# Copying the scan's output gates out of PSUM before their sigmoid and product

## The chip, the cores and the metric

The kernel runs on one core of a Trainium2 chip. Time is what one execution takes on the device, in microseconds (us). The engines are TensorE (PE, its weight loads PEld), VectorE (DVE), ScalarE (ACT), GpSimd (POOL), and SyncE (SP), which here issues transfers.

## The reference

Two blocks of two layers each work on 512 tokens of width 1024 (and 256 context tokens). What the change touches is the gated linear attention of the second block. Cut to that:

```python
def gla_scan(q, k, v, g, s0):              # once forwards, once backwards
    def step(s, inp):                      # chunks of 128 tokens
        qc, kc, vc, gc = inp
        b = jnp.cumsum(gc, axis=2)
        inter = einsum('bhtd,bhde->bhte', qc * exp(b), s)
        att = einsum('bhtd,bhsd,bhtsd->bhts', qc, kc, exp(rel))
        o = inter + einsum('bhts,bhse->bhte', att, vc)
        ...
y_gla = gla_finish(ol_f + flip(ol_b), o_norm) * jax.nn.silu(g_g)     # g_g = h @ w_in[..., 2336:2848]
m = (jax.nn.sigmoid(ga) * (ya @ w_br_attn)
     + jax.nn.sigmoid(gg) * (yg @ w_br_gla)
     + jax.nn.sigmoid(gs) * (ys @ w_br_sgu))
```

The output gate is silu(g_g) = g_g * sigmoid(g_g), with g_g of 512 features, which are four tiles of 128 features in each layer. The merge gates ga, gg and gs are of 1024 features each.

## The kernel before, in words

Activations lie with features on partitions and tokens in columns: 768 columns in the first of the second block's layers (called layer 0, `L = 0`), 512 in the second (`L = 1`). A projection tile is 128 output features. Its weights arrive by a transfer into one of three `stage` buffers, ACT rounds them to a high half (`whi`, `Weights.hi`, L198), and DVE takes the rest as a low half (`wlo`, `Weights.lo`, L212). PE then runs three products of 8 matmuls for each stretch of columns (high by U high, high by U low, low by U high; L388). The rounding runs four tiles ahead, so the rounding that belongs to a step waits (`w_used`) until PE is through with this step's own tile.

`Banks` gives out PSUM by the program's order. A claim makes PE wait until the event named by the claimant before has happened in the same banks. During the scan, banks 0 to 5 go to the scan's own products (two groups of three banks, `trio`), and every projection tile gets the one slot that is left, banks 6 and 7. So a projection tile can start only when the tile before it has been read out.

The scan of each layer (`pe_gla`, `act_gla`, `dve_gla`, `pool_gla`) works for `f` = 0, 1 (a pair of heads each) through seven levels `lv`. For a level, DVE and POOL take differences (L1884, L1965), ACT takes their exponentials (L1780), DVE and POOL multiply with q and k (L1890, L1972), PE multiplies the two (the `g0t,g0ts` matmuls, with g1 in layer 1), and DVE places the result under a mask (L1900). Between the levels' matmuls on PE lies a *step*, a projection tile that has nothing to do with the scan and fills PE's time. `scan_steps` lays down which tile stands at which place. There are 24 steps in a layer:

- 20 *fill steps* (merge gates). ACT rounds the weight tile ahead, copies the result from PSUM to the one buffer `FS` (L1717, event `fill`) and sends it to DRAM (`GS`, event `spill`). The next projection waits for `fill`.
- 4 *gate steps*, at levels 2 and 4 of each `f`, with the output gates. ACT rounds the weight tile ahead, then applies the sigmoid from PSUM (L1713, event `g_sig`), and DVE multiplies it with the same PSUM tile (L1728, event `g_gate`). The next projection waits for `g_gate`.

PE's order is level, step, level, step. Behind the matmuls of a step stand the matmuls of the next level in other banks, and only then the next step's. The product `g0g` / `g1g` is read only when `f` is finished (L1914).

Of the kernel before, what the change touches and what calls it, by code (L numbers as in the profile page):

```python
# [11 lines left out]
ALU = mybir.AluOpType  # L12
ACT = mybir.ActivationFunctionType
# [14 lines left out]
def _layout():  # L28
# [19 lines left out]
SHARED = {event: kind for kind, events in {  # L48
    "u_hi": ("n_hi", "m_uhi", "e_hi"), "u_lo": ("n_lo", "m_ulo", "e_lo"),
    "y_hi": ("f_hi", "s_yhi", "g_yhi", "q_yhi", "v_yhi"), "y_lo": ("f_lo", "s_ylo", "g_ylo", "q_ylo", "v_y"),  # L50
    "h_new": ("res", "b_add", "e_r", "h_final"), "evicted": ("m_qk", "s_qk", "q_z", "fill", "g_qk", "g_af", "v_x"),
    "modulated": ("n_mul", "u_mod"), "gain": ("n_gain", "u_gain"), "rows_act": ("m_va", "g_va"),
    "rows_dve": ("m_vd", "g_vd", "s_v", "q_v"), "v_norm": ("v_blo", "v_st", "v_ag", "v_rr", "v_n", "v_n1", "v_n2"),
    "qk_norm": ("q_rr", "q_nz"), "sigmoid": ("cb_sig", "cb_moved", "b_sig", "q_gs", "v_sig", "g_sig", "m_o"),
# [12 lines left out]
class Signals:  # L67
# [13 lines left out]
    def up(self, name, *key, by=1):  # L81
        kind = SHARED.get(name, name)
        self.count[kind] = self.count.get(kind, 0) + by
        if self.built:
            assert self.value[(name,) + key] == self.count[kind], (name, key)
        else:
            assert (name,) + key not in self.value, (name, key)
            self.value[(name,) + key] = self.count[kind]
        return self.handle(name), by

    def dma(self, name, *key):
        return self.up(name, *key, by=16)

    def at(self, name, *key):
        return self.handle(name), self.value[(name,) + key] if self.built else 1
# [127 lines left out]
def scan_steps():  # L223


    places = [("kd", m) for m in range(4)]
    for f in range(2):
        places += [("lv", f, lv) for lv in range(7)] + [("end", f, i) for i in range(3)]
    early = [(tag, j) for tag in "gas" for j in range(8)]
    tiles, gates = {}, {}  # L230
    for place in places:
        if place[0] == "lv" and place[2] in (2, 4):
            tiles[place] = ("p_gg", 2 * place[1] + place[2] // 4, None)
        else:
            n = len(gates)
            tag, j = early[n]
            gates[(tag, j)] = n
            tiles[place] = ("p_m" + tag, j, n)
    return tiles, gates


STEPS, EARLY = scan_steps()


def weight_plan():
# [62 lines left out]
def trunk_kernel(nc, A, out, stop=None):  # L308
    ctx = ExitStack()
    with ctx:  # L310
# [9 lines left out]
        def wide(name, offset, n=TOK):  # L320
            return place(name, [128, n], F32, offset)[:, :]
# [32 lines left out]
        def T(name, i):  # L354
            return number[(name, i)]

        S = Signals(lambda name: ctx.enter_context(nc.semaphore("s_" + name)))
        up, dma, at = S.up, S.dma, S.at
        B = Banks(S, PS)
        W = Weights(S, [A[name][i, :, :] for name, i in plan], plan, stage, parts)  # L360
# [41 lines left out]
        def pe_tile(pe, i, s, x, nk, full, sub=0, width=128, xt=None):  # L402
            wh, wl = W.views(i, nk)
            if sub == 0:
                pe.wait_ge(*at("w_lo", i))
            last = None
            if xt:
                for k in range(nk):
                    pe.wait_ge(*at(*xt[k]))
                    for a, b in cols(full):  # L410
                        for q, (xr, wv) in enumerate(((0, wh), (1, wh), (0, wl))):
                            last = mm(pe, s[:, a:b], wv[:, k, sub:sub + 128], x(xr, k, a, b), k + q == 0,
                                      k == nk - 1 and q == 2)
                return last
            for a, b in cols(full):
                n = 0
                for xr, wv in ((0, wh), (1, wh), (0, wl)):
                    for k in range(nk):
                        last = mm(pe, s[:, a:b], wv[:, k, sub:sub + 128], x(xr, k, a, b), n == 0, n == 3 * nk - 1)
                        n += 1  # L420
            return last

        def pe_proj(pe, i, x, full, *until, xt=None):
            s = B.take(pe, i, *until)
            pe_tile(pe, i, s, x, 8, full, xt=xt).then_inc(*up("w_used", i))
# [107 lines left out]
        def dve_lo(dve, used, n=4):  # L533
            W.lo(dve, used, dve_modulation(dve), n)
# [1008 lines left out]
        GL = [Scan(0), Scan(1)]  # L1543
# [4 lines left out]
        def pe_gla(pe, L):  # L1548
# [117 lines left out]
            def roots(f):  # L1666

                s = B.pair(pe, 1 - f, ("g_roots", L, f), ("g_rt", L, f, 1))
                for hh in range(2):
                    r = g_root(L, f, hh)  # L1670
                    B.where[("root", r)] = B.where[("g_roots", L, f, hh)]
                    pe.wait_ge(*at("g_sqo", L, f, hh))
                    for c in range(G.nc):
                        last = mm(pe, s[:, hh, c:c + 1], G.QB[:, hh, 128 * c:128 * c + 128], ONES[:, 0:1], c == 0, True)
                    last.then_inc(*up("root_sum", r))
                pe_step(pe, L, ("end", f, 1))
                pe.wait_ge(*at("root_rec", g_root(L, f, 1)))
                for c, cs, hh, rows, opens in pair_blocks():
                    last = mm(pe, s[:, hh, cs], root_cols(g_root(L, f, hh))[:, c:c + 1].to_broadcast([128, 128]), IDENT,
                              opens, True)  # L1680
                last.then_inc(*up("root", g_root(L, f, 1)))
# [18 lines left out]

        def pe_step(pe, L, step):
            name, j, n = STEPS[step]
            pe_proj(pe, T(name + str(L), j), xU, L == 0, ("g_gate", L, j) if n is None else ("fill", L, n))

        FS = wide("FS", offZ + 34912)

        def act_step(act, L, step):
            name, j, n = STEPS[step]
            i, N = T(name + str(L), j), GL[L].N
            W.hi(act, i)  # L1710
            act.wait_ge(*at("w_used", i))
            if n is None:
                act.activation(GL[L].G[j // 2][j % 2][:, 0:N], B.of(i)[:, 0:N], ACT.Sigmoid).then_inc(*up("g_sig", L, j))  # L1713
            else:
                if n or L:
                    act.wait_ge(*(at("spill", L, n - 1) if n else at("spill", 0, len(EARLY) - 1)))
                act.activation(FS[:, 0:N], B.of(i)[:, 0:N], ACT.Copy).then_inc(*up("fill", L, n))  # L1717
                act.wait_ge(*at("fill", L, n))
                act.dma_start(GS[L, n, :, 0:N], FS[:, 0:N]).then_inc(*dma("spill", L, n))

        def dve_step(dve, L, step):
            name, j, n = STEPS[step]
            dve_lo(dve, T(name + str(L), j))
            if n is None:
                i, N = T(name + str(L), j), GL[L].N
                y = GL[L].G[j // 2][j % 2][:, 0:N]
                dve.wait_ge(*at("g_sig", L, j))
                dve.tensor_tensor(y, y, B.of(i)[:, 0:N], ALU.mult).then_inc(*up("g_gate", L, j))  # L1728

        def act_gla(act, L):  # L1730
            G = GL[L]
# [1229 lines left out]
```

## Time and profile before

| | |
|---|---|
| median of 3 runs | 3404.61 us (3398.12 to 3415.74) |
| profiled execution, its own time | 3406.66 us |
| its span | 3404.9 us |
| its mean granted clock of TensorE | 0.962 |
| PE, DVE, ACT busy | 91%, 56%, 35% of the span |
| scan of layer 0, first to last level | about 1889 to 2140 us |
| scan of layer 1 | about 2828 to 3000 us |

The span is the profiled time from the first to the last instruction, the time is what the device took for that execution. Rows name PSUM as PS, the tile buffers by their names, and the line that recorded the instruction. Projection matmuls are those with `U` and `whi` or `wlo`.

### The profile page before, as it was taken

Reading aid. Unit: us, or ns where it says so; the run is one execution under the profiler, and the core shown is the slowest. Engines: PE = TensorE matmul, PEld = TensorE weight load, DVE = VectorE, ACT = ScalarE, POOL = GpSimd, SP = SyncE. Lnnn points to the kernel's source line nnn. Section 1 sums busy time; section 2 is a strip of 40 time slices with the busy share of each in tenths; the row PEclk is TensorE's granted clock in tenths of the full one; section 3 lists DMA queues with packets and bytes.
Section 4 is the critical chain, followed back from the end, with each engine's and each line's share of the span. In section 5 each row is a group of like instructions: output and inputs, shape, how many; then the busy total and the mean of one; then the engine's idle time right before and its main releaser. Section 6 shows DMA issues by size and latency. Waiting matters only on the chain.

```text
span 3404.9 us, 43105 instructions
## 1 busy us (share of the span) xinstructions
PE 3108.3 (91%) x17878; PEld 2574.3 (76%) x17878; DVE 1914.2 (56%) x2796; ACT 1180.5 (35%) x1795; POOL 210.3 (6%) x138
## 2 busy tenths in 40 slices
PE   7997889999999788999989899988999998998898
PEld 6877778888886666777877788865788776776677
DVE  7856646656434574777644543457354645455655
ACT  4225342212223454322243333325222543433432
POOL 0003100000010000000000320000000202200000
PEclk9999899999998899999989999999999999999999
DMA  5554123333321002555432222310213222230123
GB/s 209 168 169 137 44 68 125 126 126 126 100 69 60 16 1 64 166 175 175 145 82 70 73 77 73 99 32 1 96 51 129 89 72 84 87 115 26 63 96 124
DMA packets 100091, 323.92 MB, mean 95 GB/s; under 512 B 14310, under 2 KB 20326, under 8 KB 98744
## 3 DMA queue, kind: packets, MB, share of 16 engines
q1 hardware_dynamic: 89812, 291.29, 26.5%
q10 hardware_dynamic: 10084, 29.87, 2.5%
q8 instruction: 142, 2.33, 0.3%
q14 instruction: 53, 0.43, 0.0%
HBM read 301.46 MB, written 19.66 MB: 94 GB/s over the span
## 4 chain that ended last, share of the span: by engine, by line
PE 75%; DVE 11%; ACT 8%; issue 4%; DMA 1%; POOL 1%; ACTq 0%; SPq 0%; DVEq 0%; POOLq 0%
PE PS L388 74%; ACT whi L198 2%; ACT Pq L1289 1%; PE PS L391 1%; DVE STs L1326 1%; ACT nt L622 1%; DVE JUNK L525 1%; DVE stage L525 1%; DVE STq L1326 1%; ACT Ps L1289 1%; DVE wlo L212 1%; DMA Ht<-in_hT 1%; ACT U L627 1%; DVE fg L734 1%; ACT FS L1717 0%
## 5 line engine op out<-in xcount | busy, mean ns | idle before, releaser
L388 PE MATMUL PS<-U,whi 128*128 128x512 f32 (+1 forms) x4992 | 1081.8, 363 | 79.1 <-DVE U L652 27.5
L388 PEld LDWEIGHTS PS<-U,whi 128*128 128x128 f32 x4992 | 839.0, 192 | 253.9 <-issue 42.9
L212 DVE TENSOR_TENSOR wlo<-stage,whi 128x1024 fp32r<-128x1024 f32 x339 | 425.6, 1257 | 995.3 <-ACT whi L198 994.7
L198 ACT ACTIVATE whi<-stage 128x1024 fp32r<-128x1024 f32 x339 | 358.2, 1057 | 1358.8 <-PE PS L388 1329.0
L388 PE MATMUL PS<-Y,whi 128*128 128x512 f32 (+1 forms) x2240 | 581.0, 363 | 22.5 <-DVE Y L736 12.9
L388 PE MATMUL PS<-U,wlo 128*128 128x512 f32 (+1 forms) x2496 | 570.0, 355 | 0.0
L388 PEld LDWEIGHTS PS<-U,wlo 128*128 128x128 f32 x2496 | 421.9, 189 | 73.7
L388 PEld LDWEIGHTS PS<-Y,whi 128*128 128x128 f32 x2240 | 395.5, 190 | 98.4 <-DVE Y L736 14.8
L388 PE MATMUL PS<-Y,wlo 128*128 128x512 f32 (+1 forms) x1120 | 366.8, 362 | 0.0
L388 PE MATMUL PS<-whi,U 128*128 128x512 f32 (+2 forms) x1152 | 326.8, 371 | 16.1 <-DVE mV L1061 6.4
L388 PEld LDWEIGHTS PS<-whi,U 128*128 128x128 f32 x1152 | 208.5, 191 | 59.7 <-issue 11.9
L388 PEld LDWEIGHTS PS<-Y,wlo 128*128 128x128 f32 x1120 | 208.0, 190 | 34.7
L388 PE MATMUL PS<-wlo,U 128*128 128x512 f32 (+2 forms) x576 | 213.1, 370 | 0.0
L525 DVE CUSTOM_DVE_ANT_0 JUNK<-stage,CB,CL 128x1024 f32<-128x1024 f32 x128 | 163.7, 1279 | 1.0 <-DMA stage<-in_ada 1.0
L525 DVE CUSTOM_DVE_ANT_0 stage<-stage,CB,CL 128x1024 f32<-128x1024 f32 x128 | 163.9, 1281 | 0.0
L388 PEld LDWEIGHTS PS<-wlo,U 128*128 128x128 f32 x576 | 110.2, 191 | 20.2
L562 POOL TENSOR_TENSOR ACC<-ACC,SQ 128x768 f32<-128x768 f32 (+1 forms) x24 | 37.6, 1567 | 1344.9 <-ACT SQ L555 1344.9
L714 ACT ACTIVATE Y<-fg 128x768 fp32r<-128x768 f32 (+1 forms) x64 | 47.3, 739 | 208.2 <-DVE fg L734 208.2
L1289 ACT ACTIVATE Pq<-PS,STq 128x768 f32<-128x768 f32 (+1 forms) x80 | 65.1, 815 | 86.4 <-DVE STq L1330 67.4
L663 DVE SCALAR_TENSOR_TENSOR Ht<-PS,MOD,Ht 128x512 f32<-128x512 f32 x120 | 75.3, 655 | 15.1 <-PE PS L388 15.1
L736 DVE TENSOR_TENSOR Y<-fg,Y 128x768 fp32r<-128x768 f32 (+1 forms) x64 | 52.8, 825 | 51.5 <-ACT Y L714 51.5
L1326 DVE TENSOR_REDUCE STq<-PS 128x1 f32<-128x768 f32 (+1 forms) x80 | 67.6, 845 | 16.1 <-PE PS L388 15.2
(432 smaller groups left out, 3116.5 us busy)
## 6 DMA issues: line engine op xcount, KB each, us to landing
stage<-in_w SPq DMA_DIRECT2D x128, 512.0 KB, 4.0
stage<-in_ada SPq DMA_DIRECT2D x80, 512.0 KB, 3.7
stage<-in_adb SPq DMA_DIRECT2D x48, 512.0 KB, 3.7
stage<-in_p_mg SPq DMA_DIRECT2D x16, 512.0 KB, 3.7
stage<-in_p_ma SPq DMA_DIRECT2D x16, 512.0 KB, 3.8
stage<-in_p_ms SPq DMA_DIRECT2D x16, 512.0 KB, 3.8
stage<-in_wo SPq DMA_DIRECT2D x16, 512.0 KB, 3.7
GS<-FS ACTq DMA_DIRECT2D x20, 384.0 KB
```

The source lines that it names most:

```text
L198: act.activation(self.parts[r % n][0], self.stage[i % len(self.stage)], ACT.Copy).then_inc(*self.S.up("w_hi", i))
L212: dve.tensor_tensor(lo, self.stage[i % len(self.stage)], hi.bitcast(F32), ALU.subtract).then_inc(*self.S.up("w_lo", i))
L388: return pe.matmul(o, l, r, start=start, stop=stop_, skip_group_check=True)
L391: return pe.transpose(o, i, IDENT[0:k, 0:k])
L525: dve.tensor_tensor_reduce(tile if v else JUNK, tile, CB[n][v], 1.0, col(("ada2_b" if b else "ada_b") + str(L), t), ALU.mult, ALU.add, MOD ...
L562: pool.tensor_tensor(ACC[:, 0:N], ACC[:, 0:N], SQ[k % 2][:, 0:N], ALU.add).then_inc(*up("sq_add", r, k))
L622: ins = act.activation(a[:, lo:hi], a[:, lo:hi], ACT.Identity, bias=mod(L, ish, k, v), scale=MU[:, 8 * v + k:8 * v + k + 1])
L663: ins = dve.scalar_tensor_tensor(HT[:, k, lo:hi], B.of(i)[:, lo:hi], mod(cur, gate, k, v), HT[:, k, lo:hi], ALU.mult, ALU.add)
L714: act.activation(Y[:, 0, k, 0:N], FB[n % 2][:, 0:N], ACT.Copy).then_inc(*up("f_hi", L, g, k))
L736: dve.tensor_tensor(Y[:, 1, k, 0:N], b, Y[:, 0, k, 0:N].bitcast(F32), ALU.subtract).then_inc(*up("f_lo", L, g, k))
L1289: act.activation(a.P[n % 2][:, h, 0:c], B.of(("a_s", a.tag, n, h))[:, 0:c], ACT.Exp, bias=nm[:, h:h + 1], scale=0.125, accum_out=sm[:, h:h ...
L1326: dve.tensor_reduce(mx[:, h:h + 1], B.of(("a_s", a.tag, n, h))[:, 0:c], AX.X, ALU.max).then_inc(*up("a_max", a.tag, n, h))
```

## The change

In a gate step ACT now first copies the tile from PSUM to `FS` (event `g_raw`), then rounds the weight tile, and then takes the sigmoid from `FS`. DVE multiplies with `FS` instead of PSUM. The next projection waits for `g_raw`, no longer for `g_gate`. Since `FS` is also the buffer of the fill steps, two waits are added on ACT: the gate's copy waits for the spill of the fill before it, and the fill behind a gate waits for that gate's product. `BEHIND` tells for each gate which fill was the last before it.

```diff
 SHARED = {event: kind for kind, events in {
     "u_hi": ("n_hi", "m_uhi", "e_hi"), "u_lo": ("n_lo", "m_ulo", "e_lo"),
     "y_hi": ("f_hi", "s_yhi", "g_yhi", "q_yhi", "v_yhi"), "y_lo": ("f_lo", "s_ylo", "g_ylo", "q_ylo", "v_y"),
-    "h_new": ("res", "b_add", "e_r", "h_final"), "evicted": ("m_qk", "s_qk", "q_z", "fill", "g_qk", "g_af", "v_x"),
+    "h_new": ("res", "b_add", "e_r", "h_final"), "evicted": ("m_qk", "s_qk", "q_z", "fill", "g_raw", "g_qk", "g_af", "v_x"),
     "modulated": ("n_mul", "u_mod"), "gain": ("n_gain", "u_gain"), "rows_act": ("m_va", "g_va"),
     "rows_dve": ("m_vd", "g_vd", "s_v", "q_v"), "v_norm": ("v_blo", "v_st", "v_ag", "v_rr", "v_n", "v_n1", "v_n2"),
     "qk_norm": ("q_rr", "q_nz"), "sigmoid": ("cb_sig", "cb_moved", "b_sig", "q_gs", "v_sig", "g_sig", "m_o"),
@@ -227,19 +227,21 @@
     for f in range(2):
         places += [("lv", f, lv) for lv in range(7)] + [("end", f, i) for i in range(3)]
     early = [(tag, j) for tag in "gas" for j in range(8)]
-    tiles, gates = {}, {}
+    tiles, gates, behind = {}, {}, {}
     for place in places:
         if place[0] == "lv" and place[2] in (2, 4):
             tiles[place] = ("p_gg", 2 * place[1] + place[2] // 4, None)
+            behind[tiles[place][1]] = len(gates) - 1
         else:
             n = len(gates)
             tag, j = early[n]
             gates[(tag, j)] = n
             tiles[place] = ("p_m" + tag, j, n)
-    return tiles, gates
-
-
-STEPS, EARLY = scan_steps()
+    return tiles, gates, behind
+
+
+
+STEPS, EARLY, BEHIND = scan_steps()
 
 
 def weight_plan():
@@ -1700,20 +1702,28 @@
 
         def pe_step(pe, L, step):
             name, j, n = STEPS[step]
-            pe_proj(pe, T(name + str(L), j), xU, L == 0, ("g_gate", L, j) if n is None else ("fill", L, n))
+            pe_proj(pe, T(name + str(L), j), xU, L == 0, ("g_raw", L, j) if n is None else ("fill", L, n))
 
         FS = wide("FS", offZ + 34912)
 
         def act_step(act, L, step):
             name, j, n = STEPS[step]
             i, N = T(name + str(L), j), GL[L].N
-            W.hi(act, i)
-            act.wait_ge(*at("w_used", i))
             if n is None:
-                act.activation(GL[L].G[j // 2][j % 2][:, 0:N], B.of(i)[:, 0:N], ACT.Sigmoid).then_inc(*up("g_sig", L, j))
+                act.wait_ge(*at("w_used", i))
+                act.wait_ge(*at("spill", L, BEHIND[j]))
+                act.activation(FS[:, 0:N], B.of(i)[:, 0:N], ACT.Copy).then_inc(*up("g_raw", L, j))
+                W.hi(act, i)
+                act.wait_ge(*at("g_raw", L, j))
+                act.activation(GL[L].G[j // 2][j % 2][:, 0:N], FS[:, 0:N], ACT.Sigmoid).then_inc(*up("g_sig", L, j))
             else:
+                W.hi(act, i)
+                act.wait_ge(*at("w_used", i))
                 if n or L:
                     act.wait_ge(*(at("spill", L, n - 1) if n else at("spill", 0, len(EARLY) - 1)))
+                for k, last in BEHIND.items():
+                    if last == n - 1:
+                        act.wait_ge(*at("g_gate", L, k))
                 act.activation(FS[:, 0:N], B.of(i)[:, 0:N], ACT.Copy).then_inc(*up("fill", L, n))
                 act.wait_ge(*at("fill", L, n))
                 act.dma_start(GS[L, n, :, 0:N], FS[:, 0:N]).then_inc(*dma("spill", L, n))
@@ -1725,7 +1735,7 @@
                 i, N = T(name + str(L), j), GL[L].N
                 y = GL[L].G[j // 2][j % 2][:, 0:N]
                 dve.wait_ge(*at("g_sig", L, j))
-                dve.tensor_tensor(y, y, B.of(i)[:, 0:N], ALU.mult).then_inc(*up("g_gate", L, j))
+                dve.tensor_tensor(y, y, FS[:, 0:N], ALU.mult).then_inc(*up("g_gate", L, j))
 
         def act_gla(act, L):
             G = GL[L]
```

ACT around the first gate step of layer 0, before. `whi_52` is a half of the weights rounded ahead, `g0g_177` is the first output gate, `g0t` and `g0ts` are a level's target and source factors.

```order
L198 ACTIVATE whi_52<-stage_50 128x1024 [waits s_w_used,s_w_in1]
L1713 ACT_TABLE_LOAD
L1713 ACTIVATE g0g_177<-PS 128x768 [waits s_w_used]
L1780 ACT_TABLE_LOAD
L1780 ACTIVATE g0t_165<-g0t_165 128x768 [waits s_target]
L1780 ACTIVATE g0ts_174<-g0ts_174 128x768 [waits s_source]
L198 ACTIVATE whi_54<-stage_51 128x1024 [waits s_w_used,s_w_in2]
L1717 ACTIVATE FS<-PS 128x768 [waits s_spilled,s_w_used]
```

The same place in the changed kernel (L1715 is the new copy, L1718 the sigmoid, L1790 the exponentials, L1727 the fill's copy).

```order
L1715 ACTIVATE FS<-PS 128x768 [waits s_spilled,s_w_used]
L198 ACTIVATE whi_52<-stage_50 128x1024 [waits s_w_used,s_w_in1]
L1718 ACT_TABLE_LOAD
L1718 ACTIVATE g0g_177<-FS 128x768 [waits s_evicted]
L1790 ACT_TABLE_LOAD
L1790 ACTIVATE g0t_165<-g0t_165 128x768 [waits s_target]
L1790 ACTIVATE g0ts_174<-g0ts_174 128x768 [waits s_source]
L198 ACTIVATE whi_54<-stage_51 128x1024 [waits s_w_used,s_w_in2]
L1727 ACTIVATE FS<-PS 128x768 [waits s_gated,s_spilled,s_w_used]
```

One copy stands ahead of the rounding, the number of table loads is the same, and the next fill's copy has one more wait (`s_gated`, the product). This occurs eight times, four in each layer.

DVE at the same place, before.

```order
L212 TENSOR_TENSOR wlo_53<-stage_50,whi_52 128x1024 [waits s_w_hi]
L1728 TENSOR_TENSOR g0g_177<-g0g_177,PS 128x768 [waits s_sigmoid]
L1884 TENSOR_TENSOR g0t_165<-g0b 128x12x32 [waits s_g_pr]
L1884 TENSOR_TENSOR g0t_165<-g0b 128x12x32
L1890 TENSOR_TENSOR g0t_173<-g0t_173,g0qk 128x768 [waits s_g_te]
L1900 COPY_PREDICATED g0att<-g0mk,PS 128x1536 [waits s_g_pl,s_g_pr]
```

And in the changed kernel.

```order
L212 TENSOR_TENSOR wlo_53<-stage_50,whi_52 128x1024 [waits s_w_hi]
L1738 TENSOR_TENSOR g0g_177<-g0g_177,FS 128x768 [waits s_sigmoid]
L1894 TENSOR_TENSOR g0t_165<-g0b 128x12x32 [waits s_g_pr]
L1894 TENSOR_TENSOR g0t_165<-g0b 128x12x32
L1900 TENSOR_TENSOR g0t_173<-g0t_173,g0qk 128x768 [waits s_g_te]
L1910 COPY_PREDICATED g0att<-g0mk,PS 128x1536 [waits s_g_pl,s_g_pr]
```

Nothing moved on DVE; its product reads `FS` in place of PSUM. The order of instructions on PE, POOL and SP is the same in both kernels.

## Rows read from the trace of the kernel before

**Rows 1.** The page: busy time by engine, and the chain that ended last.
```profile
PE 3108.3 (91%) x17878; PEld 2574.3 (76%) x17878; DVE 1914.2 (56%) x2796; ACT 1180.5 (35%) x1795; POOL 210.3 (6%) x138
...
PE 75%; DVE 11%; ACT 8%; issue 4%; DMA 1%; POOL 1%; ACTq 0%; SPq 0%; DVEq 0%; POOLq 0%
```
**Rows 2.** The product's line, L1728: who waited for it (us, times).
```profile
  PE PS L388: 22.1, 8
```
**Rows 3.** Timeline, layer 0, a fill step; start and length in us, idle before in brackets.
```profile
1918.32 0.79 ACT L1717 ACTIVATE FS<-PS 128x768 f32<-128x768 f32 x1
...
1919.16 3.99 PE L388 MATMUL PS<-U,whi 128*128 128x512 f32 x16 [0.37 <-ACT FS L1717]
```
**Rows 4.** Timeline, layer 0, the first gate step.
```profile
1927.75 1.61 PE L388 MATMUL PS<-g0t,g0ts 64*128 64x128 f32 x24
1927.92 1.06 ACT L198 ACTIVATE whi<-stage 128x1024 fp32r<-128x1024 f32 x1 [4.43 <-PE PS L388]
1928.99 1.28 ACT L1713 ACT_TABLE_LOAD   x1
...
1929.52 2.31 POOL L1965 TENSOR_TENSOR g0ts<-g0b 128x384 f32<-128x384 f32 x2 [4.04 <-PE PS L388]
1930.29 0.81 ACT L1713 ACTIVATE g0g<-PS 128x768 f32<-128x768 f32 x1
...
1931.13 0.95 DVE L1728 TENSOR_TENSOR g0g<-g0g,PS 128x768 f32<-128x768 f32 x1 [0.90 <-ACT g0g L1713]
...
1932.14 4.00 PE L388 MATMUL PS<-U,whi 128*128 128x512 f32 x16 [2.78 <-DVE g0g L1728]
1932.94 0.95 DVE L1890 TENSOR_TENSOR g0t<-g0t,g0qk 128x768 f32<-128x768 f32 x1
...
1940.73 1.61 PE L388 MATMUL PS<-g0t,g0ts 64*128 64x128 f32 x24
```
**Rows 5.** Timeline, layer 1, the first gate step.
```profile
2851.16 1.16 PE L388 MATMUL PS<-g1t,g1ts 64*128 64x128 f32 x16
2851.33 1.06 ACT L198 ACTIVATE whi<-stage 128x1024 fp32r<-128x1024 f32 x1 [2.55 <-PE PS L388]
...
2855.07 5.55 PE L388 MATMUL PS<-U,whi 128*128 128x512 f32 x16 [2.75 <-DVE g1g L1728]
2855.60 0.69 DVE L1890 TENSOR_TENSOR g1t<-g1t,g1qk 128x512 f32<-128x512 f32 x1
...
2856.25 0.61 ACT L1780 ACTIVATE g1ts<-g1ts 128x512 f32<-128x512 f32 x1
```
**Rows 6.** Timeline, layer 1, behind a fill step, and behind the second gate step.
```profile
2845.36 4.00 PE L388 MATMUL PS<-U,whi 128*128 128x512 f32 x16 [0.60 <-ACT FS L1717]
...
2873.87 3.99 PE L388 MATMUL PS<-U,whi 128*128 128x512 f32 x16 [2.75 <-DVE g1g L1728]
...
2879.66 1.16 PE L388 MATMUL PS<-g1t,g1ts 64*128 64x128 f32 x16
```
**Rows 7.** Timeline, behind the first and the last of five gate steps alike.
```profile
2048.46 5.54 PE L388 MATMUL PS<-U,whi 128*128 128x512 f32 x16 [2.78 <-DVE g0g L1728]
...
2958.22 5.41 PE L388 MATMUL PS<-U,whi 128*128 128x512 f32 x16 [2.75 <-DVE g1g L1728]
```
**Rows 8.** Stretches with fill steps only, and behind a gate step: PEclk is third from the end.
```profile
1966.00:2045.00 79.00, 77.59 (x560) 68.58 (x562) 35.45 (x35) 26.93 (x34) 18.73 (x13) 1.00 0.24 82
2050.00:2052.00 2.00, 2.00 (x6) 1.56 (x5) 2.00 (x2) 0.95 (x2) 0.91 (x1) 0.50 0.00 0
```
**Rows 9.** The line that copies a tile to FS: ns min/median/max.
```profile
L1717 ACT ACTIVATE FS<-PS x40: 577/686/802, 1852.1 to 2998.9; 128x768 f32<-128x768 f32 x20, 128x512 f32<-128x512 f32 x20
```
**Rows 10.** Timeline, layer 0, VectorE and GpSimd on two products at once.
```profile
1895.25 2.02 POOL L1972 TENSOR_TENSOR g0ts<-g0ts,g0qk 128x768 f32<-128x768 f32 x1
1895.51 2.57 DVE L1890 TENSOR_TENSOR g0t<-g0t,g0qk 128x768 f32<-128x768 f32 x1
```
**Rows 11.** DMA while a tile of layer 1 is spilled: share and GB/s stand last.
```profile
2850.00:2851.00 1.00, 1.00 (x6) 0.65 (x4) 0.00 (x0) 0.00 (x0) 0.22 (x1) 1.00 0.00 0
```

## The prediction

> **What bounds the kernel now.** I read the page first. PE is busy for 91% of the span, and 75% of the chain that ended last is PE [rows 1]. So an idle stretch of PE in this kernel is worth its length, if what fills it does not wait for the same thing. Next I read who waits for the line that the change unties, the product of the output gate (L1728): PE, eight times, 22.1 us in total [rows 2]. Then I read the timeline around one step of each kind, to see what releases PE.
>
> In a fill step ACT rounds and copies (1918.32 to 1919.11) under the next level's matmuls, and the next projection starts at 1919.16, after 0.37 us of idleness [rows 3]. In a gate step the level's matmuls run from 1927.75 to 1929.36 and the rounding starts at 1927.92, but behind it come a table load of 1.28 us, the sigmoid of 0.81 and the product of 0.95, in a chain. The product ends at 1932.08 and the projection starts at 1932.14, after 2.78 us of idleness [rows 4]. Layer 1 has the same picture with 512 columns: level 2851.16 to 2852.32, projection at 2855.07, 2.75 us idle [rows 5]. Four gates of 2.78 and four of 2.75 make 11.1 + 11.0, the 22.1 of [rows 2]. PE's next work in order is that projection, so nothing else hides this.
>
> There is a second loss behind the gap. The first 16 matmuls of the next projection take 3.99 or 4.00 us behind fill steps and behind three of the gate steps [rows 3, 4, 6], but 5.4 to 5.55 us behind the five others [rows 5, 7]. The granted clock tells why. It is 1.00 of 2.4 GHz in 79 us with fill steps only, although these have a gap of 0.37 us in every step, and 0.50 (1.2 GHz) in the 2 us that I looked at behind a gate step of the five [rows 8]. A fall costs 5.55 - 4.00 = 1.55 us, the last one 1.42 [rows 5 to 7].
>
> **The change part by part.** *Removed from PE's wait: rounding, table load, sigmoid, product. Put in its place: one copy.* The price of the copy is that of the fill's copy, 0.79 us for 768 columns in the timeline [rows 3] and 0.58 us (577 ns, the least of the line) for 512 [rows 9]. It waits for the same event as the rounding did, so it starts where the rounding started. Layer 0: 1927.92 + 0.79 = 1928.71, which is 0.65 before the level's matmuls end at 1929.36 [rows 4]. Layer 1: the rounding started at 2851.33, so 2851.33 + 0.58 = 2851.91, 0.41 before 2852.32 [rows 5]. With the 0.05 from the copy's end to the matmul's start [rows 3], the copy stays under the level's matmuls in both, and PE is idle for nothing. What hides it is the level's matmuls of 1.61 and 1.16 us; without them the copy would cost 8 times 0.7 us. So the whole idle time goes, 22.1 us [rows 2]. A gate step then has even less of a gap than a fill step.
>
> *The clock.* No gap of 2.75 us is left there, and steps with gaps of 0.37 us kept the full clock for 79 us [rows 8]; behind one of 0.60 in layer 1 it was full too [rows 6]. I take all five falls as gone: 4 x 1.55 + 1.42 = 7.6 us. The other bound is nothing, if falls come at other places instead.
>
> *Added to ACT:* eight copies, 4 x 0.79 + 4 x 0.58 = 5.5 us on an engine that is 35% busy [rows 1]. What stands behind them is later by one copy (0.79 or 0.58): rounding, sigmoid, product, and the exponentials and differences behind these. Who waits for that? PE's next level needs DVE's factor (L1890). In layer 0 it ends at 1932.94 + 0.95 = 1933.89 and will end at 1934.7. The level will be due at 1929.36 + (1940.73 - 1932.14) = 1937.95 [rows 4], so 3.3 us are left. In layer 1 it ends at 2856.29, will end at 2856.9, and is due at 2852.32 + (2879.66 - 2873.87) = 2858.1, so 1.2 us are left [rows 5, 6]. That is the tightest place, and it occurs twice (level 2 of each `f`). Cost nothing, up to 1.2 us of delay. The rounded weights are used four steps later and are not late.
>
> *Sigmoid and product from memory.* Products of the same shape from memory take 0.95 us (L1890), like the product from PSUM [rows 4]; I take no difference. But there is a price that PSUM spared: where GpSimd was at work from 1895.25 to 1897.27, a VectorE product of two tiles in memory took 2.57 us instead of 0.95, that is 1.62 more, and it ended 0.81 after GpSimd's [rows 10]. In the gate steps GpSimd works from 1929.52 to about 1931.8 [rows 4], and the new product starts at 1931.1 + 0.8 = 1931.9, so it just misses that. If it is hit in full, VectorE is late by 1.62 more, which only the two tight places feel: 2 x (1.62 - 1.2) = 0.8 us. I put it at nothing. The Trainium skill's GPSIMD Engine Reference, section Key points, says that GpSimd shares its SBUF interfaces with VectorE and contends with instructions of two SBUF inputs, which the product now becomes. By that rule the sum would be 0.8 us less gain, and the rows above agree that the contention is real.
>
> *The added waits.* The gate's copy waits for the spill before it. The spill is issued when the fill's copy ends, which in layer 1 is what the projection at 2845.36 waited for [rows 6], and the gate's copy comes at 2851.33, some 6.0 us later. The DMA engines are idle from 2850 to 2851 [rows 11], so the spill has landed. The bounds are nothing and, if a spill were later by 1 us there, 4 x (1 - 0.36) = 2.6 us (0.36 is what the copy has to spare under the level). I take nothing. The fill behind a gate waits for the product, which ends near 1932.9, while its own matmuls end near 1938. Nothing.
>
> *A rule against the change.* After the table load the sigmoid starts at once: 1928.99 + 1.28 = 1930.27, and it started at 1930.29 [rows 4]. The Trainium skill's ScalarE: Activation LUTs, section What ACT_TABLE_LOAD costs, adds a drain of about 1.38 us to each switch, 2.66 in all. If that came to be paid here, ACT would be late for the fill behind a layer 1 gate by 2 x 1.38 less the 0.8 us of slack (rival 2), that is by 2 us at each of two places, 4 us in all, an estimate from that page; the trace shows no such drain.
>
> *Sum.* 22.1 + 7.6 = 29.7 us. The profiled execution took 3406.66 us, so it becomes 3377.0. The median shown lies 2.05 us lower, so 3374.9. With 1 us for the small terms (bounds 0.8 and 2.6), I say 3376.
>
> **The rivals.**
> 1. *The gap closes, the clock's falls do not go away* (or new ones come elsewhere). For it: the whole span has a granted clock of 0.962, so there are many other falls, and where they come shifts with every microsecond; three runs of the same kernel differ by 17.6 us. Against it: in 79 us of fill steps there is no fall [rows 8]. Then 22.1 us: 3382.5.
> 2. *A part of the wait comes back.* Either VectorE's chain is late for the level, or ACT is late for the next fill. After a gate in layer 1, ACT was through with the exponentials at 2856.25 + 0.61 = 2856.86 and will be at 2857.5, and the next rounding is due 0.17 behind the level's start, near 2858.3 [rows 5]; that is 0.8 us of slack. If contention or late transfers take 1 us of each gate, 8 us of the gain go: about 3384 with the clock's part, 3391 without.
> 3. *Slower.* VectorE becomes the bound at the gate steps: lo half, product and differences each blocked by GpSimd. Each block costs at most 1.62 us [rows 10], three make 4.9. The layer 1 slack is 1.2, the layer 0 slack 3.3, so PE would wait 3.7 and 1.6 us: 4 x 5.3 = 21 us, against 22.1 gained. It decides above 5 us of delay a gate, with a few more falls of the clock on top. It would give about 3406, or up to 3425 with two falls a gate step (16 x 1.2). Against it: GpSimd has two instructions in this stretch, not three, and two gates of each layer (level 4) have no differences behind the product.
> 4. *No effect*, because the projection behind a gate waited for something else as well that ends as late. Against it: PE's start follows the product's end by 0.06 us in [rows 4], and the weights were rounded four steps before. 3404.
>
> **How the numbers follow.** Chances: forecast 0.66, rival 1 0.18, rival 2 0.09, rival 3 0.03, rival 4 0.04. About 0.5% (17 us, that is 3387.6) is what a measurement of this kernel can tell from no change. The forecast and most of rival 1 lie beyond it, rival 2 in part: faster 0.84. Rivals 4 and the rest of 2: same 0.13. Rival 3: slower 0.03. The range takes in the forecast with the scatter of the runs (the three reach 6.5 below and 11.1 above their median): 3376 - 11 = 3365 at the low end. At the high end it reaches over rival 1 with its scatter to the 3391 of rival 2 without the clock's part.
>
> **What would show it.** Right: PE's idle time before the projection behind each gate is nothing, or below 0.1 us; the wait for the product is gone from PE's list; the copies show 0.79 and 0.58 us; the first 16 matmuls there take 4.0 us in all eight; the scans are shorter by 11.1 plus 3.1 us and 11.0 plus 4.5 us. Wrong: a new wait of PE for L1727 (the next fill's copy) over 0.6 us, or for the factor (L1890 before, L1900 in the changed kernel) at the level behind a gate; a copy that starts later than 0.2 us after the level's matmuls began, which means a spill that has not landed; a product of 2.5 us, which is the contention; or the same count of slow stretches of the clock elsewhere. The forecast is wrong as a whole if the scans are shorter but the span is not, that is, if a later stage gives the time back.

## The result

| | before | changed |
|---|---|---|
| median | 3407.28 us (14 runs, 3398.12 to 3422.18) | 3389.98 us (14 runs, 3382.69 to 3401.37) |
| ratio to before | | 0.9946 (0.9933 to 0.996) |
| profiled execution | 3406.66 us | 3399.3 us |
| its span, its mean granted clock | 3404.9 us, 0.962 | 3397.5 us, 0.956 |

The change gains 17.3 us by the medians, 18.4 by the ratio. 29.7 were forecast. Measured again it was 3389.28 against 3406.59, ratio 0.9951 (0.9932 to 0.9969).

The wait did what the forecast said. This is who PE waits for in the changed kernel, from 1890 to 2090 us and from 2815 to 2990 us, the scans of the two layers (us, times, longest):

```profile
PE PS L390 <- DVE g0t L1900: 3.7, 1, 3.7
PE PS L390 <- ACT FS L1727: 3.3, 9, 0.4
```

```profile
PE PS L390 <- DVE g1t L1900: 6.8, 1, 6.8
PE PS L390 <- ACT FS L1727: 5.4, 9, 0.6
```

The product (L1738 now) is gone from the lists; before, it stood for the 22.1 us of [rows 2]. The two waits for a factor (L1900) stand ahead of the first level of each scan, and the kernel before has the same 3.7 and 6.8 us there. The timeline around the first gate step of layer 0, which answers to [rows 4]:

```profile
1928.29 1.61 PE L390 MATMUL PS<-g0t,g0ts 64*128 64x128 f32 x24
1928.39 0.81 ACT L1715 ACTIVATE FS<-PS 128x768 f32<-128x768 f32 x1 [4.38 <-PE PS L390]
1929.10 1.05 ACT L198 ACTIVATE whi<-stage 128x1024 fp32r<-128x1024 f32 x1
...
1929.82 3.99 PE L390 MATMUL PS<-U,whi 128*128 128x512 f32 x16
1930.05 2.60 POOL L1975 TENSOR_TENSOR g0ts<-g0b 128x384 f32<-128x384 f32 x2 [4.05 <-PE PS L390]
1930.17 1.28 ACT L1718 ACT_TABLE_LOAD   x1
1930.18 1.78 DVE L212 TENSOR_TENSOR wlo<-stage,whi 128x1024 fp32r<-128x1024 f32 x1 [5.09 <-ACT whi L198]
1931.46 0.85 ACT L1718 ACTIVATE g0g<-FS 128x768 f32<-128x768 f32 x1
...
1932.34 1.12 DVE L1738 TENSOR_TENSOR g0g<-g0g,FS 128x768 f32<-128x768 f32 x1 [0.38 <-ACT g0g L1718]
...
1934.32 0.94 DVE L1900 TENSOR_TENSOR g0t<-g0t,g0qk 128x768 f32<-128x768 f32 x1
...
1938.41 1.61 PE L390 MATMUL PS<-g0t,g0ts 64*128 64x128 f32 x24
```

The copy starts 0.10 us behind the level's start and ends at 1929.20, the level at 1929.90, and the projection follows without a gap (its row has no bracket). The clock stays up: the first 16 matmuls take 3.99 us. In layer 1, which answers to [rows 5]:

```profile
2844.71 0.60 ACT L1715 ACTIVATE FS<-PS 128x512 f32<-128x512 f32 x1 [2.48 <-PE PS L390]
...
2845.69 4.00 PE L390 MATMUL PS<-U,whi 128*128 128x512 f32 x16
...
2849.51 0.68 DVE L1900 TENSOR_TENSOR g1t<-g1t,g1qk 128x512 f32<-128x512 f32 x1
...
2851.49 1.16 PE L390 MATMUL PS<-g1t,g1ts 64*128 64x128 f32 x16
```

The factor (L1900) ends at 2850.19, 1.3 us before its level. All eight first groups of 16 behind gates take 3.99 or 4.00 us.

So where did the rest go? Both traces have the same PE program, so one can follow how far the changed kernel is ahead, by the start of the same rounding on ScalarE in both. Before, at the end of layer 0's scan and behind the value projection of the attention:

```profile
2132.12 1.06 ACT L198 ACTIVATE whi<-stage 128x1024 fp32r<-128x1024 f32 x1 [2.80 <-PE PS L388]
...
2213.69 1.06 ACT L198 ACTIVATE whi<-stage 128x1024 fp32r<-128x1024 f32 x1 [7.13 <-PE PS L388]
...
2233.73 1.06 ACT L198 ACTIVATE whi<-stage 128x1024 fp32r<-128x1024 f32 x1 [16.62 <-PE PS L388]
```

The changed kernel at the same three roundings:

```profile
2119.76 1.06 ACT L198 ACTIVATE whi<-stage 128x1024 fp32r<-128x1024 f32 x1 [2.80 <-PE PS L390]
...
2201.34 1.06 ACT L198 ACTIVATE whi<-stage 128x1024 fp32r<-128x1024 f32 x1 [7.11 <-PE PS L390]
...
2233.91 1.06 ACT L198 ACTIVATE whi<-stage 128x1024 fp32r<-128x1024 f32 x1 [29.15 <-PE PS L390]
```

At the end of the scan it is 12.36 us ahead, and still at the second row. At the third it is 0.18 behind. It had been 0.53 behind ahead of the scan (1906.76 and 1907.29), so the scan gained 12.9 us and one tile lost 12.5. In layer 1 it is 6.6 us ahead before the scan, 22.3 behind it (15.6 gained), and 9.5 behind the value projection (12.8 lost). The 6.8 us between the tile of layer 0 and the scan of layer 1 were gained from 2726 us on, where the kernel before spends 10.2 us more at 0.50, and another 2.1 us were lost behind the last tile; the edit touches neither place. The balance is the 7.4 us between the two spans. The stretches of that projection, changed kernel, PEclk third from the end:

```profile
2208.00:2232.00 24.00, 24.00 (x114) 24.00 (x114) 4.65 (x5) 0.00 (x0) 0.00 (x0) 0.50 0.00 1
2236.00:2240.00 4.00, 3.80 (x12) 2.20 (x11) 3.96 (x8) 0.90 (x1) 0.00 (x0) 0.74 0.42 131
3042.00:3066.00 24.00, 24.00 (x115) 24.00 (x114) 1.94 (x4) 0.00 (x0) 0.00 (x0) 0.50 0.00 1
```

And in the kernel before:

```profile
2218.00:2233.00 15.00, 15.00 (x137) 15.00 (x136) 7.01 (x5) 0.00 (x0) 0.00 (x0) 1.00 0.05 22
3061.00:3076.00 15.00, 15.00 (x137) 15.00 (x136) 5.18 (x5) 0.00 (x0) 0.00 (x0) 1.00 0.07 28
```

The value projection is 144 matmuls of 128x128. At 1.00 it is through in 16.3 us; in the changed kernel the clock fell to 0.50 within 2.5 us of its start and stayed there for 30.7 us, which is to the end of the tile and about 4 us beyond, into matmuls of 128x512. The falls behind the gate steps lasted 3.4 us each in the trace of the kernel before. Nothing in this tile was changed. PE waits 1.6 us (layer 0) and 1.8 to 1.9 us (layer 1) ahead of it in both kernels.

The traced executions of the changed kernel are at the slow end of its runs: 3399.3 us here, and 3401.43, the slowest of six, in the repetition below. The quicker runs have a higher mean granted clock (0.961 and 0.962 at 3383.81 and 3382.69 us, 0.956 at 3399.3). So the quicker executions probably had fewer stuck tiles; they were not traced.

### The profile page after: what moved, and what is told of

Read it like the earlier page. It is cut to its first block, busy times and chain, and to the rows that moved or that the text cites. A ratio compares the mean times of both kernels' runs of the same rounds, so it can differ in the third digit from the quotient of the medians.

```text
span 3397.5 us, 43121 instructions
## 1 busy us (share of the span) xinstructions
PE 3130.6 (92%) x17878; PEld 2596.2 (76%) x17878; DVE 1914.4 (56%) x2796; ACT 1186.3 (35%) x1803; POOL 210.1 (6%) x138
## 4 chain that ended last, share of the span: by engine, by line
PE 76%; DVE 10%; ACT 7%; issue 4%; DMA 1%; POOL 1%; ACTq 0%; SPq 0%; DVEq 0%; POOLq 0%
PE PS L390 75%; ACT whi L198 1%; PE PS L393 1%; ACT Pq L1291 1%; DVE STs L1328 1%; ACT nt L624 1%; DVE JUNK L527 1%; DVE stage L527 1%; DVE STq L1328 1%; DVE wlo L212 1%; ACT Ps L1291 1%; DMA Ht<-in_hT 1%; ACT U L629 1%; DVE fg L736 1%; ACT FS L1727 0%
## 5 line engine op out<-in xcount | busy, mean ns | idle before, releaser
L390 PE MATMUL PS<-Y,whi 128*128 128x512 f32 (+1 forms) x2240 | 581.0, 363 | 22.4 <-DVE Y L738 12.9
L390 PE MATMUL PS<-whi,U 128*128 128x512 f32 (+2 forms) x1152 | 349.2, 390 | 13.5 <-DVE mV L1063 6.4
L390 PEld LDWEIGHTS PS<-whi,U 128*128 128x128 f32 x1152 | 227.2, 211 | 56.6 <-issue 11.9
L390 PE MATMUL PS<-wlo,U 128*128 128x512 f32 (+2 forms) x576 | 223.7, 388 | 0.0
L390 PEld LDWEIGHTS PS<-wlo,U 128*128 128x128 f32 x576 | 121.3, 211 | 20.0
```

Source lines behind the costliest of these rows:

```text
L390: return pe.matmul(o, l, r, start=start, stop=stop_, skip_group_check=True)
```

## The experiments

"Value projection" is that tile, and it is "stuck" when the clock falls in it and stays down to its end, "free" when it runs at 1.00 throughout. A trace also records when the granted clock changed. Within each of the thirteen traces the changes lie on one regular grid of times, to 3 ns; where the grid lies against the kernel's own start differs from trace to trace. "Start" is how long behind the last point of that grid the value projection began, worked out from these records.

**Two repetitions (e1, e2).** No edit.

> The changed kernel once more, for a second trace and more times. In its first trace PE waited for no gate product, the two scans were shorter by 12.9 and 15.7 us, but TensorE's granted clock was 0.50 for 30.7 us in each layer during the value projection of the attention (144 matmuls of 128x128), which cost 12.5 and 12.8 us and was not there in the trace of before. Theory C (chance): whether the clock stays low in that stretch differs from execution to execution in both kernels, so this trace can show none, one or two such stretches, and the time goes with their number, some 12.6 us each. Rival T (tied to the change): both stretches are at 0.50 here too, in every trace of the changed kernel. Time against before by both: 15 to 23 us shorter.

> The kernel before once more, for a second trace. Theory C: long stretches at 0.50 in the value projection can occur here as well, with a chance like that of the changed kernel. Rival T: none, as in its first trace. Time against before: ratio 1.000 within 0.2%.

Measured: e1 3389.28 us (ratio above), e2 3407.24 us, ratio 0.9997 (0.9985 to 1.001). In e1's trace the value projection is stuck in both layers again. In e2's it is free in layer 0 and stuck in layer 1. The matmuls of this tile, e2 (min/median/max in ns):

```profile
L388 PE MATMUL PS<-whi,U x96: 273/274/300, 2220.5 to 2236.3; 128*128 128x128 f32 x96
...
L388 PE MATMUL PS<-whi,U x96: 273/415/415, 3054.9 to 3083.8; 128*128 128x128 f32 x96
```

A median of 274 ns is the full clock, 415 the half. So it can happen in the kernel before (1 of 4 traced), and rival T, which had it impossible there, is out. It happened in all 4 of the changed one; four against one is too few to rule out chance (C), and the next pair was built for that.

**Wide matmuls in its place (e3, e4).** The values of this tile are not computed. The edit, shortened:

```diff
+        def pe_rows_wide(pe, key, i, until):
...
+            for t in range(6):
+                o = B.of((key, t // 2))[:, 512 * (t % 2):512 * (t % 2) + 512]
+                for m in range(12):
+                    last = mm(pe, o, wh[:, m % 8, :], xU(0, m % 8, 0, 512), m == 0, m == 11)
...
-                    pe_rows(pe, ("q_v", L), [T(f"p_av{L}", 0)], xU, 6, 128, lambda j: (("q_v", L, 2 * j + 1),))
+                    pe_rows_wide(pe, ("q_v", L), T(f"p_av{L}", 0), lambda j: (("q_v", L, 2 * j + 1),))
```

> The changed kernel, with the 144 matmuls of 128x128 of the attention's value projection replaced by 72 matmuls of 128x512 in the same PSUM banks, about as long (72 x 0.235 = 17 us against 16.2). The values are not those of the reference. Behind wide matmuls the clock always came back within 3 to 17 us in the traces, so a long stretch at 0.50 should be gone. If the stuck clock is what took the forecast gain back, this kernel is shorter than the changed one by 10 to 12 us on average (one stretch an execution), near 3379, and its times scatter less. If something else took it, it stays near 3390.

> The same replacement in the kernel before. The difference of this one and the one above is the change without the stuck stretches. Forecast's theory (22.1 us of waiting and up to 7.6 of clock): 22 to 30 us. Theory C, in which both kernels lose as much to those stretches on average: this kernel is as much shorter than before as the one above is than the changed kernel, and the pair differs by the same 18 us as the originals. Rival T: this kernel is within 2 us of before and the pair differs by some 28 us.

Measured: e3 3370.96 us (3369.83 to 3374.93), ratio 0.9897 (0.9882 to 0.9913). e4 3406.95 us, ratio 1.0002 (0.9992 to 1.0012). The kernel before loses nothing measurable to this tile, the changed one 18 us, which is more than the 10 to 12 I expected. Without it the pair is 36.0 us apart, so the gain was made and was taken back here; it is also above the 30 us that I had as the most. Theory C is out: it expected both to become shorter. (Of the four wide tiles traced, one had a fall, for 3.4 us.)

**Moving the start (e5, e6, e11).** Matmuls of 128x512 are added ahead of the attention's first projection, and their result is overwritten. The edit, shortened:

```diff
+                    for m in range((10, 9)[L]):
+                        mm(pe, s[:, 0:512], wh[:, m % 8, :], xU(0, m % 8, 0, 512), True, True)
+                    pe_tile(pe, i, s, xU, 8, G.wide_at(0)).then_inc(*up("w_used", i))
```

This is e5, with 10 in layer 0 and 9 in layer 1. e6, on the kernel before, has `(4, 4)[L]`, and e11, on the changed one, `(0, 9)[L]`.

> The changed kernel with work added: 10 matmuls of 128x512 in layer 0 and 9 in layer 1 (2.3 and 2.1 us), whose result is overwritten, ahead of the first projection of the attention. Position theory (P): whether the value projection runs at 0.50 depends on when it starts against the clock's possible changes, and the change moved that start; in four traces it stayed at full clock where it began 0.1 to 0.3 us behind such a point and fell where it began 1.0 to 1.9 us behind one. The pad moves the start near the harmless place, so the 30.7 us at 0.50 go in both layers: time shorter than the changed kernel by 10 to 20 us in spite of 4.4 us more work, that is 3370 to 3380. Rival T (something in the changed kernel itself, its later rounding or its use of FS, holds the clock down): still stuck, 3389 + 4 = 3393 or more.

> The kernel before with 4 such matmuls (0.93 us) in each layer at the same place. Theory P: in layer 0 the value projection now starts about 1.1 us behind a possible change of the clock in place of 0.1 to 0.3, where the changed kernel's fell, so that it runs at 0.50 for 30.7 us in most executions: 1.9 + 12.5 us longer in layer 0 alone, 3418 to 3425. Rival T: 1.9 us longer, 3408.

> The changed kernel with 9 matmuls of 128x512 (2.1 us) ahead of the attention's first projection in layer 1 alone. With 10 and 9 in both layers (e5) layer 1's value projection kept the full clock and layer 0's did not. Position theory: layer 1 is spared its 12.6 us again and layer 0 is as in the changed kernel, so 12.6 - 2.1 = 10.5 us below the changed kernel's 3389: 3379, faster with more work. If the position had nothing to do with it: 3391.

Measured: e6 3433.1 us (3429.07 to 3434.7), ratio 1.0075 (1.0063 to 1.0088): 1.9 us of work cost 25.1, more than I expected, since layer 1 was caught too. e5 3391.86 us, ratio 0.9957 (0.9944 to 0.9969). e11 3377.4 us, ratio 0.99 (0.9881 to 0.9918): by the medians 12.6 us below the changed kernel with 2.1 us more work. The tile's matmuls in e6, layer 0 and layer 1:

```profile
L388 PE MATMUL PS<-whi,U x96: 273/415/415, 2222.3 to 2250.8; 128*128 128x128 f32 x96
...
L388 PE MATMUL PS<-whi,U x96: 273/415/415, 3075.2 to 3103.4; 128*128 128x128 f32 x96
```

In e5:

```profile
L390 PE MATMUL PS<-whi,U x96: 274/415/420, 2207.1 to 2236.5; 128*128 128x128 f32 x96
...
L390 PE MATMUL PS<-whi,U x96: 273/274/300, 3047.7 to 3063.6; 128*128 128x128 f32 x96
```

In e11:

```profile
L390 PE MATMUL PS<-whi,U x96: 273/274/297, 2203.6 to 2219.4; 128*128 128x128 f32 x96
...
L390 PE MATMUL PS<-whi,U x96: 273/274/300, 3033.1 to 3049.0; 128*128 128x128 f32 x96
```

e6 is stuck in both layers, e5 in layer 0 alone, e11 in neither. e5 missed for layer 0: the pad of 2.3 us was to bring the start from 1.0 round to the next point of the grid, and it came to 2.4. Some 0.3 us of the miss is that the tile began only 2.05 us later than in the changed kernel's trace, and 0.7 that the grid lay elsewhere against the program. And e11 came out right in part by luck: its layer 0 has no pad and runs what the changed kernel runs, yet in this trace it started at 0.11 and was free, where I had it stuck. The starts of all traces with the original form of the tile:

| | kept the full clock | stuck at 0.50 |
|---|---|---|
| kernel before | 0.13, 0.07, 0.31 (e2) | 1.87 (e2) |
| changed | 0.11 (layer 0 of e11) | 1.03, 1.33, 1.04 (e1), 1.72 (e1) |
| with pads | 0.00 (e5), 0.22 (e11) | 2.41 (e5), 1.41, 1.02 (e6) |

Six starts up to 0.31 kept it, eight from 1.02 on did not; none fell between. The kernel before and the changed one stand in both columns, and a 0.93 us pad makes the kernel before 25 us slower. So the place in time decides, not the gate steps' new form.

**The wait taken away (e7, e8).** The tile's three pairs of banks are claimed one by one. All values are computed. The edit, shortened; the function that it replaces takes all three ahead of its first matmul:

```diff
+        def pe_rows_lazy(pe, key, i, x, until):
...
+            for t in range(6):
+                if t % 2 == 0:
+                    B.take(pe, (key, t // 2), *until(t // 2))
...
-                    pe_rows(pe, ("q_v", L), [T(f"p_av{L}", 0)], xU, 6, 128, lambda j: (("q_v", L, 2 * j + 1),))
+                    pe_rows_lazy(pe, ("q_v", L), T(f"p_av{L}", 0), xU, lambda j: (("q_v", L, 2 * j + 1),))
```

> The changed kernel, in which the value projection claims its three pairs of PSUM banks one by one as it comes to them, instead of all three ahead of its first matmul. The wait of 1.6 and 1.8 us for ScalarE's root, which stands ahead of it, is then covered by the first 48 to 96 of its matmuls. All values are computed. If the fall of the clock needs that wait, both long stretches at 0.50 go and so does the wait: 3.4 us and one to two times 12.6 us, 3365 to 3378. If narrow matmuls alone pull the clock down, only 3.4 us: 3386.

> The same in the kernel before. By theory P 3.4 us and the occasional stuck stretch (one in four layers traced) go: 3398 to 3403. The pair of this and the one above then shows the change without the stuck clock: forecast 29.7 us, at least 22.

Measured: e7 3367.05 us (3361.95 to 3367.66), ratio 0.9879 (0.9864 to 0.9894). e8 3400.79 us, ratio 0.9978 (0.9966 to 0.9991). The stretch of the tile in e7, layers 0 and 1:

```profile
2200.00:2220.00 20.00, 18.69 (x153) 17.28 (x151) 10.67 (x10) 4.62 (x6) 0.00 (x0) 1.00 0.09 27
3022.00:3040.00 18.00, 17.54 (x149) 16.65 (x147) 7.47 (x7) 3.21 (x5) 0.00 (x0) 1.00 0.10 30
```

The clock is 1.00 in both, and so it is in all eight traced tiles of this form (e7 to e10), though they started at 0.44 to 2.35 behind a point of the grid, six of the eight at 1.00 or later. So the stuck clock needs the wait ahead of the narrow matmuls as well as the bad start; the narrow matmuls alone do not pull the clock down. e7 is 1.2% faster than the kernel before and the best version here. The pair e7 and e8 is the change without the stuck clock: 33.7 us. It is more than the forecast's 29.7 because the falls behind gates are more than five on average: the traces of the kernel before and of its variants have 5, 4 (e2), 6 (e4), 8 (e6) and 8 (e8), that is 31 in 40 gate steps. Those with the copy (after, e1, e3, e5, e7, e9, e11) have none in 56.

**Which part of the gate step's edit carries it (e9, e10).** e9 is e7 with the copy behind the rounding. e10 is e8 without any copy, with the sigmoid ahead of the rounding and the product ahead of the low half, both from PSUM. The edits, shortened:

```diff
--- e7
+++ e9, gate step
+                W.hi(act, i)
                 act.wait_ge(*at("w_used", i))
                 act.wait_ge(*at("spill", L, BEHIND[j]))
                 act.activation(FS[:, 0:N], B.of(i)[:, 0:N], ACT.Copy).then_inc(*up("g_raw", L, j))
-                W.hi(act, i)
--- e8
+++ e10, gate step, ACT and then DVE
-            W.hi(act, i)
-            act.wait_ge(*at("w_used", i))
             if n is None:
+                act.wait_ge(*at("w_used", i))
                 act.activation(GL[L].G[j // 2][j % 2][:, 0:N], B.of(i)[:, 0:N], ACT.Sigmoid).then_inc(*up("g_sig", L, j))
+                W.hi(act, i)
...
-            dve_lo(dve, T(name + str(L), j))
                 dve.tensor_tensor(y, y, B.of(i)[:, 0:N], ALU.mult).then_inc(*up("g_gate", L, j))
+            dve_lo(dve, T(name + str(L), j))
```

> The changed kernel with the late claims (run e7), and the gate's copy behind the rounding of the weight tile, as in a fill step, in place of ahead of it. My theory of the wait: PE then waits 0.37 us behind a layer 0 gate and 0.60 behind a layer 1 gate, as behind a fill, 4 x 0.37 + 4 x 0.60 = 3.9 us more than e7's 3367: 3371. So nearly all of the gain is the copy itself, not its place ahead of the rounding. Rival (the place ahead of the rounding carries the gain, since the rounding is 1 us): 8 us more, 3375.

> The kernel before with the late claims (run e8), and no copy: the sigmoid stands ahead of the rounding on ScalarE and the product ahead of the low half on VectorE, both still from PSUM. The wait for the product should shrink from 2.78 and 2.75 to 1.7 us, by 8 x 1.07 = 8.6 us, to 13.6 us in total. If the clock's falls behind the gates follow the wait's length, some of them go too and the time is more than 8.6 us below e8's 3400.8: 3385 to 3392. If they don't, 3392.

Measured: e9 3374.23 us, ratio 0.9891 (0.9872 to 0.991). e10 3372.11 us, ratio 0.9883 (0.9864 to 0.9901). PE's waits in e9, layer 0 and layer 1, L1729 being the gate's copy:

```profile
PE PS L390 <- ACT FS L1729: 1.5, 4, 0.4
...
PE PS L390 <- ACT FS L1729: 2.4, 4, 0.6
```

They are 1.5 + 2.4 = 3.9 us, as I expected. The time is not: 3374.2 is nearer to the rival's 3375 than to my 3371, and the medians of e7 and e9 differ by 7.2. In the traces the two kernels are already 4.4 us apart at 1304 us, ahead of anything that was edited, so only some 4 us seem to be the edit's. The ratios say the same (0.0012, about 4 us), though their intervals overlap. So it is the waits that decide for my theory, not the time. e10 was better than I thought. Its first gate step of layer 0:

```profile
1921.28 1.28 ACT L1725 ACT_TABLE_LOAD   x1
...
1925.53 1.61 PE L388 MATMUL PS<-g0t,g0ts 64*128 64x128 f32 x24
1925.64 0.81 ACT L1725 ACTIVATE g0g<-PS 128x768 f32<-128x768 f32 x1 [3.07 <-PE PS L388]
1926.34 1.05 ACT L198 ACTIVATE whi<-stage 128x1024 fp32r<-128x1024 f32 x1
1926.48 0.96 DVE L1742 TENSOR_TENSOR g0g<-g0g,PS 128x768 f32<-128x768 f32 x1 [4.13 <-ACT g0g L1725]
...
1927.49 4.00 PE L388 MATMUL PS<-U,whi 128*128 128x512 f32 x16 [0.35 <-DVE g0g L1742]
```

With nothing between the exponential and the sigmoid, ScalarE loads the table at 1921.28, while it still waits for PE, and not in PE's wait. The wait is 0.35 us, not the 1.7 I had worked out with the load inside. No gate step is followed by a fall. By the medians e10 is 28.7 us below e8, with 19.4 us less waiting, so the reordering alone gives most of the gain. What the copy adds to that is not settled: e7 is 5.1 us below e10 by the medians and PE waits 2.7 us less in it, but by the ratios (0.9879 and 0.9883) it is 1.4 us and their intervals overlap.

## Why the prediction was right, and where it was off

- *The wait of 22.1 us goes, in all eight gate steps.* Right, to the tenth. The copies took 0.81 and 0.60 us where 0.79 and 0.58 were taken, and hid under the level's matmuls.
- *Five falls of the clock behind gates, 7.6 us, go.* Right at the place: none of the eight gate steps has one. The scans became shorter by 12.9 and 15.6 us where 14.2 and 15.5 were worked out; in layer 0 the changed kernel has a new fall of 3.4 us in the middle of the scan, from 1988.9 us on, behind no gate. As a measure of an average execution 7.6 was small: over all traces with the old order 31 of 40 gate steps have a fall, not 5 of 8.
- *VectorE's chain keeps 1.2 us at the tightest place.* Right, 1.3. The contention with GpSimd is there, and now with numbers: the low half took 1.78 us in place of 1.23 and the product 1.12 in place of 0.95. The prediction had the product just miss GpSimd's work; it overlapped by 0.3 us (GpSimd until 1932.65, the product from 1932.34). PE waited for none of it. So the rule of the Trainium skill's GPSIMD Engine Reference, section Key points, holds here and costs nothing. The other rule weighed there, the drain of 1.38 us behind a table load in ScalarE: Activation LUTs, section What ACT_TABLE_LOAD costs, shows in neither kernel: the load at 1930.17 took 1.28 us and the sigmoid started at 1931.46.
- *The spill has landed, the next fill waits for nothing new.* Right; the waits for the fill's copy were the same 3.3 and 5.4 us.
- *The clock's term, +7.6 with 0 as its other bound (and so rival 1, with 22.1 us).* This is the step that failed. "The other bound is nothing, if falls come at other places instead": I priced a fall anywhere at what it costs between wide matmuls, 1.55 us, and so took the clock to be worth between 0 and +7.6. The one place behind the scans where PE waits and then runs narrow matmuls only costs 12.5 to 12.8 us when the clock falls there. The change moved the program by 12.4 us at the tile of layer 0 and by 22.3 at that of layer 1, and in both its traces the two tiles began on the harmful side. The term should have read: +7.6 at the gates, and 0 to -25 behind them. With the forecast's 29.7 that spans 3377 to 3402, which is where the runs lie (3382.69 to 3401.37). The median had 16.4 us taken back (33.7 - 17.3). That is 1.3 stuck tiles of 12.6, an estimate from these rows, where the traced executions had two.
- *The last sign of being wrong that it names, "a later stage gives the time back".* It came true in the trace: of the 28.5 us that the scans gained, 25.3 were given back right behind them.
- The direction held. The range (3365 to 3391) held by one microsecond, and that is luck: its upper end was set for other reasons, and both traced executions (3399.3 and 3401.43) lie outside it. Rival 3 also prices a fall at 1.2 us where the rest of the text has 1.55; its upper end would be 3431, and nothing hangs on it.

What stays open: why a wait and a late start together keep the clock down; only that both are needed is shown. Also what sets the start in an execution. The changed kernel's layer 0 began at 1.03 and 1.04 in two traces, but at 0.11 in e11's with the same program up to there, and the layer 1 of the kernel before at 0.07 and 1.87. So a pad cannot be counted on to put the tile where it does no harm; taking the wait away can.

## What to carry to other kernels

A wait that a chain of other engines sets between two bursts of matmuls can be cut by moving the reader of PSUM ahead of work that nobody waits for; look first whether a mere reordering does it, and whether a table load then falls into idle time. When a change moves the program in time, list the stretches of narrow matmuls that begin with a wait of PE: in this kernel that is where the granted clock fell and did not come back, and claiming PSUM banks only when they are needed took the wait away. Where runs of one kernel scatter by 0.5%, read the granted clock of the stages before crediting a difference to the edit.

## What was not expected of the hardware

- TensorE's granted clock, once at 0.50 in a stretch of 144 matmuls of 128x128 back to back, stayed there for 30.7 us (34.1 once, in e5), with PE busy all through the tile, at 415 ns a matmul for 274. In the same form of stretch without a wait ahead of it (e7 to e10, eight tiles) it never fell.
- 0.93 us of added matmuls in each layer cost 25 us (e6).
- The Trainium skill's TensorE: Matmul & The Clock Gate, Part 1, says that the throttled state is the default and that activity releases it. By the row of 2208 to 2232 us PE was busy for 24.00 of 24 us at 0.50 and nothing was released, so here the measurement decides: in this tile being busy was not enough.
- A table load is carried out ahead of the wait of the activation that needs it, 4.4 us early in e10.
- A copy that was queued first on ScalarE started 0.10 us behind the level's first matmul (1928.39 and 1928.29), where the rounding started 0.17 behind it [rows 4].
